# First norm computed by token, first gate unit tile by tile, first loads issued by two engines, and three shifts of convolution tile 2 moved from the matrix engine to the vector engine

## The reference, cut to what matters

```python
h = rmsnorm(x, norm_mix[0])                     # x * rsqrt(mean(x*x) + 1e-6) * g
a = jnp.einsum("bsd,de->bse", h, w_pw1) + b_pw1 # 1024 -> 2048
u = a[..., :d] * jax.nn.sigmoid(a[..., d:])     # value half, gate half
u = causal_dwconv(u, w_dw, b_dw)                # depthwise, 31 taps
u = jax.nn.silu(layernorm(u, ln_g, ln_b))
x = x + jnp.einsum("bsd,de->bse", u, w_pw2) + b_pw2
```

## Time and profile before

| | before |
|---|---|
| executions shown | 951.72, 952.87, 952.91 us, median 952.87 |
| the profiled execution's own time | 952.73 us, with a span of 950.9 us |
| mean granted TensorE clock | 0.994 of full speed |
| busy, share of the span | PE 938.1 us (99%), DVE 554.9 (58%), ACT 388.6 (41%), POOL 112.7 (12%) |
| instructions | 11880 |
| HBM read, written | 86.09 MB, 2.10 MB |

### The profile page before, as it was taken

How to read it: one execution, slowest core, us unless ns; L and a number is a source line. 1 busy time by engine, 2 the same in 40 slices (tenths; PEclk the granted TensorE clock), 3 DMA queues, 4 the chain that set the end, 5 groups by cost and what they waited for, 6 DMA issues and landing times.

```text
span 950.9 us, 11880 instructions
## 1 busy us (share of the span) xinstructions
PE 938.1 (99%) x4496; PEld 790.2 (83%) x4496; DVE 554.9 (58%) x711; ACT 388.6 (41%) x597; POOL 112.7 (12%) x74
## 2 busy tenths in 40 slices
PE   8999999999999999999999999999999999999996
PEld 6889898888888888888888898888888888888886
DVE  6899995657555555564434459765555555532333
ACT  7785596434334333342322355433343333322220
POOL 0558896000000000000000020000000000000000
PEclk9999999999999999999999999999999999999998
DMA  7320022232222223312222341232222232222212
GB/s 254 114 89 1 1 90 89 89 99 109 103 88 88 88 88 102 118 61 91 87 96 91 117 155 45 94 124 91 88 88 88 90 111 80 83 86 104 91 62 89
DMA packets 17020, 88.56 MB, mean 93 GB/s; under 512 B 2016, under 2 KB 4320, under 8 KB 9952
## 3 DMA queue, kind: packets, MB, share of 16 engines
q1 hardware_dynamic: 16416, 87.67, 27.0%
q10 hardware_dynamic: 576, 0.52, 0.2%
HBM read 86.09 MB, written 2.10 MB: 93 GB/s over the span
## 4 chain that ended last, share of the span: by engine, by line
PE 97%; DVE 1%; DMA 1%; ACT 0%; SPq 0%; issue 0%; DVEq 0%
PE bank L1127 29%; PE bank L1128 28%; PE bank L1129 28%; PE bank L1178 2%; PE bank L1180 2%; PE bank L1179 2%; PE bank L1469 1%; DMA x_res<-x 1%; DVE out_sb L1117 1%; PE bank L1196 0%; PE bank L1437 0%; PE bank L1442 0%; PE bank L1441 0%; PE bank L1202 0%; PE bank L1240 0%; PE bank L1230 0%
## 5 line engine op out<-in xcount | busy, mean ns | idle before, releaser
L1127 PE MATMUL bank<-h_hi,w_hi 128*128 128x512 f32 x800 | 312.4, 390 | 0.0
L1129 PE MATMUL bank<-h_hi,w_lo 128*128 128x512 f32 x800 | 311.4, 389 | 0.0
L1128 PE MATMUL bank<-h_lo,w_hi 128*128 128x512 f32 x800 | 311.3, 389 | 0.0
L455 ACT ACTIVATE w_hi<-w_raw 128x2048 fp32r<-128x2048 f32 (+2 forms) x87 | 147.3, 1693 | 211.9 <-PE bank L1129 211.9
L764 DVE TENSOR_TENSOR w_lo<-w_raw,w_hi 128x2048 fp32r<-128x2048 f32 (+2 forms) x81 | 162.1, 2002 | 100.6 <-ACT w_hi L455 99.8
L1127 PEld LDWEIGHTS bank<-h_hi,w_hi 128*128 128x128 f32 x800 | 150.2, 188 | 31.7 <-issue 0.5
L1128 PEld LDWEIGHTS bank<-h_lo,w_hi 128*128 128x128 f32 x800 | 150.2, 188 | 31.6 <-issue 0.5
L1129 PEld LDWEIGHTS bank<-h_hi,w_lo 128*128 128x128 f32 x800 | 150.2, 188 | 31.1
L1128 PE MATMUL bank<-u_lo,w_hi 128*128 128x512 f32 (+1 forms) x406 | 153.3, 378 | 0.0
L1127 PE MATMUL bank<-u_hi,w_hi 128*128 128x512 f32 (+1 forms) x374 | 141.1, 377 | 0.4 <-DVE w_lo L764 0.4
L1129 PE MATMUL bank<-u_hi,w_lo 128*128 128x512 f32 (+1 forms) x374 | 140.8, 377 | 0.0
(11 more groups left out here) (208 smaller groups left out, 996.1 us busy)
## 6 DMA issues: line engine op xcount, KB each, us to landing
w_raw<-w_up SPq DMA_DIRECT2D x44, 1024.0 KB, 4.8
w_raw<-w_down SPq DMA_DIRECT2D x32, 704.0 KB, 4.1
w_raw<-w_pw SPq DMA_DIRECT2D x11, 1024.0 KB, 4.9
x_res<-x SPq DMA_DIRECT2D x3, 512.0 KB, 8.0
out<-out_sb SPq DMA_DIRECT2D x12, 128.0 KB, 1.8
w_raw<-w_pw SPq DMA_DIRECT2D x4, 256.0 KB, 7.7
w_raw<-w_pool SPq DMA_DIRECT2D x2, 512.0 KB, 3.5
band_raw<-band SPq DMA_DIRECT2D x1, 800.0 KB, 5.5
```

The lines of the kernel that those rows point to most:

```text
L455: nc.scalar.activation(w_hi[s][:, 0:columns], w_raw[s][:, 0:columns], ACT.Copy).then_inc(w_rounded[s], 1)
L1127: M.matmul(dst, a, hi, start=start, stop=False)
L1128: M.matmul(dst, a, lo, start=False, stop=False)
L1129: return M.matmul(dst, b, hi, start=False, stop=stop)
```

## The change

- **Loads.** ACT now issues x tiles 0, 2 and 3 (as three loads of one tile; 2 and 3 were one load before) and parts 2 and 3 of unit 0; SP keeps `par`, parts 0 and 1, x tile 1, tiles 4 and 5, 6 and 7, unit 1 and the rest.
- **First norm.** The eight squares are added as a tree of five instructions (two of them 1024 columns wide). PE sums by blocks (`sum_wide`), ACT takes the root of four columns, DVE inverts four columns, and PE spreads the factors over the partitions (`spread_blocks`) into bank 5, from where ACT copies them to `rms`.
- **Second unit.** `second_unit` finishes gate tile 0 first, then gate tile 1, with the sum and the spread inside the latter. DVE drains and multiplies tile by tile.
- **Moved work.** The split of unit 0 of step 1 goes from DVE to POOL, the pool vectors from DVE to POOL, and ACT's `tap_columns` behind the first two sigmoids. `clear_sums` at the start is gone.
- **Tile 2.** The first `SOONER_SHIFTS` = 3 shifts of tile 2 become six taps on DVE (the last of 256 columns), added to the tile by one instruction; PE leaves them out of units 0 and 1. `conv_unit(2)` and one sum of POOL wait for that addition.
- **Order on DVE.** The numbers of taps between the drains are changed.

```diff
+SOONER_TILE, SOONER_SHIFTS, BANK_SOONER = 2, 3, 1
...
             sp.dma_start(par[:, 0:N_FIRST], vecs[:, 0:N_FIRST]).then_inc(par_loaded, 16)
-            load_x(0, 0, 1)
             load_part(0)
             load_x(1, 1, 2)
-            load_x(2, 2, 4)
             load_part(1)
-            load_x(3, 4, 6)
-            load_part(2)
-            load_part(3)
-            load_x(4, 6, 8)
+            load_x(4, 4, 6)
+            load_x(5, 6, 8)
...
-            pool.wait_ge(w_split[0], M_PW1 + 2)
+            pool.wait_ge(summed, KD + 1)
+            split(0, M_PW1 + 1)
+            split(1, M_PW1 + 1)
...
+            load_x(0)
             act.wait_ge(consts_set, CONSTS)
-            nc.scalar.activation(warm[:, :], eps[:, 0:1], ACT.Copy)
+            nc.scalar.activation(warm[:, 0:1], eps[:, 0:1], ACT.Copy)
+            load_x(2)
+            load_x(3)
+            load_part(2)
+            load_part(3)
...
+            touch_root()
+            act.wait_ge(stat_mm, 1)
+            nc.scalar.activation(root_tok[:, :], bank[BANK_SUM][:, 0:T:P], ACT.Sqrt, scale=1.0 / D, bias=eps[:, 0:1]).then_inc(root_done, 1)
+            nc.scalar.activation(warm[:, 1:2], eps[:, 0:1], ACT.Sigmoid)
...
+            act.wait_ge(first_spread, 1)
+            nc.scalar.activation(rms[:, :], bank[BANK_FIRST][:, :], ACT.Copy).then_inc(first_read, 1)
+            first_sigmoid(0)
+            first_sigmoid(1)
+            round_unit(1, M_PW1 + 1, UNIT)
             tap_columns()
-            round_unit(1, M_PW1 + 1, UNIT)
-            sigmoid(0)
...
-            add_square(0)
-            add_square(1)
             split_unit(1, M_PW1, UNIT)
-            for c in range(2, KD):
-                add_square(c)
-            split_unit(0, M_PW1 + 1, UNIT)
-            inverse(0)
+            add_squares(0)
+            add_squares(1)
+            dve.wait_ge(in_added, 4)
+            V.tensor_tensor(sumsq[:, :], in_sq[:, 0, :], in_sq[:, 4, :], ADD).then_inc(summed, KD + 1)
+            dve.wait_ge(root_done, 1)
+            V.reciprocal(root_tok[:, :], root_tok[:, :]).then_inc(rms_ready, 1)
...
             scale_val(3)
-            taps(1, 8, 15)
+            taps(1, 8, 13)
             drain_gate(3)
-            taps(1, 15, 16)
+            taps(1, 13, 14)
             multiply(3)
...
-            taps(1, 16, 24)
+            taps(1, 14, 24)
...
+                if u == 2:
+                    pe.wait_ge(sooner_added, 1)
+                first = {SHARED_TILE: SHARED_SHIFTS, SOONER_TILE: SOONER_SHIFTS}.get(CONV_TILES[n], 0)
...
+            def second_unit():
+
+
+                pe.wait_ge(w_rounded[1], 1)
+                for t in range(2):
+                    dst = bank[BANKS_PW1[0][1] + t][:, :]
+                    for k in range(KD):
+                        if (t, k) == (1, 1):
+                            pe.wait_ge(summed, KD + 1)
+                            sum_wide(sumsq, start=True, stop=True).then_inc(stat_mm, 1)
+                        if (t, k) == (1, 5):
+                            pe.wait_ge(ident_loaded, 16)
+                            pe.wait_ge(rms_ready, 1)
+                            spread_blocks(bank[BANK_FIRST], root_tok, range(BLOCKS)).then_inc(first_spread, 1)
```

More of the change, by code:

```diff
@@ L92 @@
 BANK_SUM, BANK_MEAN = 4, 7
+BANK_FIRST = 5
 BANK_IDLE = 3
@@ L145, in build @@
         pool_shift = place("pool_shift", [P, KD], f32)
-        warm = place("warm", [P, 1], f32)
+        warm = place("warm", [P, 2], f32)
         start_sum = place("start_sum", [P, START], f32)
@@ L888, in _ @@
+            dve.wait_ge(first_read, 1)
+            dve.wait_ge(first_gate, 1)
+            first_gate_drain(0)
+            scale_val(0)
+            first_multiply(0)
+            tap(0, 0, 0)
+            tap(0, 0, 1)
+            dve.wait_ge(unit_done[1], 1)
+            first_gate_drain(1)
+            tap(0, 0, 2)
+            first_multiply(1)
+            for k in range(3):
+                tap(0, 1, k)
+            taps(0, 3, 8)
             scale_val(1)
-            taps(0, 8, 13)
+            taps(0, 8, 15)
@@ L890, in _ @@
             drain_gate(1)
-            taps(0, 13, 15)
+            taps(0, 15, 17)
             multiply(1)
-            taps(0, 15, 20)
+            taps(0, 17, 21)
             scale_val(2)
-            taps(0, 20, 24)
+            taps(0, 21, 28)
             drain_gate(2)
-            taps(0, 24, 26)
+            taps(0, 28, 30)
             multiply(2)
-            taps(0, 26)
-            taps(1, 0, 8)
+            taps(0, 30)
+            for k in range(2 * SOONER_SHIFTS):
+                sooner_tap(k)
+                taps(1, k, k + 1)
@@ L1241, in first_unit @@
                 last.then_inc(unit_done[0], 1)
-            def first_norm(k):
-                if k == 5:
-                    sum_channels(0)
+            def second_unit():
[10 more added lines that the diff above has]
+                            spread_blocks(bank[BANK_FIRST], root_tok, range(BLOCKS)).then_inc(first_spread, 1)
+                        a = w_hi[1][:, (2 * k + t) * P:(2 * k + t + 1) * P]
+                        M.matmul(dst, a, h_hi[:, k, :], start=k == 0, stop=False)
+                        M.matmul(dst, a, h_lo[:, k, :], start=False, stop=False)
+                    pe.wait_ge(w_split[1], 1)
+                    for k in range(KD):
+                        last = M.matmul(dst, w_lo[1][:, (2 * k + t) * P:(2 * k + t + 1) * P], h_hi[:, k, :], start=False, stop=k == KD - 1)
+                    last.then_inc(first_gate if t == 0 else unit_done[1], 1)
             def second_norm(k):
@@ L1282, in wait_free @@
                     wait_drained((2, 3), DRAINED_PW1 + {(2, 0): 1, (3, 1): 3}[i, s])
-            for i in range(PW1_STEPS):
-                for s in range(0 if i else 1, 2):
+            second_unit()
+            for i in range(1, PW1_STEPS):
+                for s in range(2):
                     wait_free(i, s)
-                    unit(s, M_PW1 + i, h_hi, h_lo, None if i else first_norm, at_bank=BANKS_PW1[i][s])
+                    unit(s, M_PW1 + i, h_hi, h_lo, at_bank=BANKS_PW1[i][s])
                 if i == 2:
```

93 lines of the change are left out of this document (61 added, 32 removed).

## The result

The changed kernel takes 955.58 us (median; 954.64 to 956.76 over 7 runs), the kernel before 952.31 us beside it (951.72 to 953.05). The ratio is 1.0035, 95% interval 1.0026 to 1.0044: **slower by 0.35%, 3.3 us**. The forecast was 951.9 us with a range up to 954.0 us, so it was wrong in size and in sign. The profiled execution of the changed kernel took 954.98 us, 2.25 us more than the profiled one of before.

The account below looks back on a forecast made before the run. PE was taken to bound the kernel, DVE close behind. The start's 1.05 and tile 2's 2.14 make 3.2 us, 2.3 given back on DVE: 0.9 gained, 951.9 us; own range 951.0 to 952.6, with rivals 950.2 to 954.0.

Parts of the forecast that it names:

- I take 16.0 us: Start: unit 1's load, which landed at 16.56 before, would land at 16.0 us; forecast range 15.1 to 16.6.
- path two: Start: unit 1's landing, ACT's rounding, DVE's split and adds lead to the sum over channels, issued at 24.9 us.
- The start gives 1.05 us: Start: `second_unit` would end at 31.7 us instead of 32.75, a gain of 1.05 us.
- My first rival: Start: loads come no earlier and PE's stall stays; sum at 26.8 us, total 953.9 us, slower; 20%.
- The second norm of the start: In `second_unit`: behind the sum's issue come 22 matmuls (5.0 us), the sum (0.9) and the spread (0.9).
- tile 2: Mixer: 18 matmuls of 256 columns leave PE, a gain of 2.14 us.
- DVE's load: Mixer: with its added taps DVE is ready near 105.1 and waits 1.5 us at the last gate drain.
- Four taps have moved behind that drain: 2.64 us ... 0.35 slack: Last gate drain to layer norm: 2.64 us more DVE work less 0.35 slack gives back 2.3 of 3.2 us.
- The clock falls in the layer norm: Layer norm: two new PE waits of 1.1 and 1.2 us lower the clock, costing 1.65 us, 953.6 us; 13%.

Follow-up runs that it names:

- experiment 1: The changed kernel with all first loads issued by SP again, in the order of before: 953.47 us, ratio 1.0018 to the kernel before.
- experiment 6: The changed kernel with one tap pair back ahead of the last gate drain, mean from PSUM, parts 2 and 3 on SP ahead of unit 1: 949.59 us.
- experiment 7: The kernel before with only the change's loads (ACT issues x tiles 0, 2, 3 and parts 2, 3): 954.46 us, ratio 1.0025.
- experiment 12: The kernel before with only x tiles 0, 2 and 3 issued by ACT, parts 2 and 3 staying on SP ahead of unit 1: 951.95 us, ratio 1.0001.
- experiment 2: The changed kernel with one pair of taps moved back ahead of the last gate drain: 955.12 us, ratio 1.0032 to the kernel before.
- experiment 3: The changed kernel with the shared tile's first tap reading the near mean from PSUM instead of SBUF: 952.81 us, ratio 1.0006 to the kernel before.
- experiment 9: The changed kernel with 14 and 7 idle matmuls ahead of PE's two new waits at the end of the mixer: 955.55 us, ratio 1.0033.
- experiment 10: The changed kernel with 8 and 4 idle matmuls ahead of PE's two new waits at the end of the mixer: 954.50 us, ratio 1.0023.
- experiment 8: The kernel before with only the mean taken from PSUM by the shared tile's first tap: 951.80 us, ratio 0.9996.
- experiment 5: The changed kernel with first loads as before, one tap pair back ahead of the last gate drain, and the mean from PSUM: 950.18 us, ratio 0.9979.

## Why the prediction was wrong

**"I take 16.0 us" for the landing of unit 1, and the step that hangs the sum on that landing alone: these failed.** Unit 1 landed at 16.55, inside the range of 15.1 to 16.6. The larger miss is that I took path two to be landing, rounding, split, adds, and left out that ACT must first round part 3 of unit 0 and x tiles 6 and 7 and square two tiles. The change had just moved part 3 into another queue, and I priced ACT's issues and the bytes of unit 1, not the landing of the small load beside it. Part 3 landed at 15.27, and ACT came to unit 1 1.5 us after its landing; the sum was issued at 26.90 instead of 24.9. Of these 2.0 us the landing is 0.55 and the wait for ACT the rest. "The start gives 1.05 us" became a loss of 1.0: 2.05 us. Experiments 1, 6, 7 and 12 show it from four sides, among them that 24.7 to 25.5 is what the same chain gives when part 3 is on time.

My first rival had the right sign and nearly the right moment of the sum (26.8 us; its total of 953.9 was 1.7 short), but another mechanism: it had PE's stall stay. So that moment was met by luck: the stall shrank, and PE waited for DVE. The Trainium skill (page "DMA: Bandwidth & Descriptors", section "Issuing engines are not separate DMA queues"), which spoke against this term, was right for unit 1, which was issued 3.4 us sooner and landed at 16.55 as before. Single loads did move: ACT rounded x tile 2 at 8.46 instead of 9.65, and x tile 1 at 7.83 instead of 5.82. The section's word that such transfers interleave is the sharper warning, and the same page's section on queues, rings and completion order says that an SDMA engine takes turns between the rings it has work for. The runs agree with that: part 3 in a queue beside x tiles 4 to 7 and unit 1 landed 11.83 us after its issue (11.2 in experiment 7), and ahead of unit 1 in one queue after 8.8 (9.0 in experiment 12).

**The second norm of the start, tile 2 and DVE's load: right.** `second_unit` itself costs what was reckoned: from the sum to the next unit 6.94 us, predicted 6.8. PE gained 2.14 less the start's loss. DVE had 1.22 us of idle time at the last drain (predicted 1.5), and the wide add took the 1.22 us taken for it.

**"Four taps have moved behind that drain: 2.64 us ... 0.35 slack": right, but not all of it.** The step treats DVE's other instructions behind the drain as unchanged. One of them waits for POOL, and the same change had shifted DVE against POOL: +0.93 us. The 1.48 us of this one tap among taps of 0.75 stood in the trace of before, and I had not asked what they were. Experiments 2 and 3 show the cause. The Trainium skill (page "SBUF — State Buffer", section "SBUF: two separate sides") states it: VectorE and GpSimd share a port pair, and a DVE instruction with two SBUF inputs and a GpSimd one that reads SBUF shut each other out for the whole instruction. The trace agrees: DVE's end stands 0.55 or 0.56 us behind POOL's in all eight kernels that keep this form (before, the change, experiments 1, 2, 7, 9, 10 and 12), wherever it began. It shows the other side too: POOL's work next behind it takes 4.08 us before, where the same takes 3.62 in experiment 8.

**"The clock falls in the layer norm": it did**, a rival with 13%. Its sign and place were right. The price of 1.65 us is not refuted: in the profiled execution of the change the stretch from the sum of squares to that of `conv_out` took 0.69 more and the maximum 0.45 less, but in experiment 1 that stretch took 1.4 more, and in experiment 2 it is 44.87 us from the last drain to the end of the maximum, 2.4 more than in the change. The wait that set it off was 1.92 us instead of 1.1, for the DVE wait had been added to it; in experiment 3, with 0.44 and 0.93, the clock held.

Missed as well, in the change's favour: the maximum with zero, 0.45 us less, which the slow clock brought with it. The four misses are 2.05 + 0.93 + 0.69 - 0.45 = 3.2 us, which is the distance between the -0.9 forecast and the +2.3 found. The cases were also treated as rivals of one another, where two of them came together with a third that had no case. That, more than any width, put 955.6 outside a range that ended at 954.0.

## What to carry to other kernels

When a small load moves to a second queue, ask what loads then run beside it, and which instruction stands behind the small one on its consumer; keep what is needed first ahead in the same queue. An instruction that takes twice its neighbours' time is a wait with a cause, and its length changes when either engine moves. A stall is worth only what the next wait leaves of it, and a wait that is free now may not stay so: DVE's for POOL cost nothing in the kernel before, and taking it away gave 2.8 us by the medians once DVE was last.

## What the runs showed that was not expected

- A DVE instruction with two SBUF tensors in fp32 takes 1.48, 2.41 or 3.79 us in place of 0.75, according to how long POOL's running instruction still lasts. With one of the two in PSUM it takes 0.75 beside the same POOL instruction.
- A DVE TENSOR_SCALAR on 4 columns shows the same: 0.62 us when it ended with POOL's split (148.81 and 148.78), 0.17 where it began within 0.1 us of that split's end or behind it. It has one tensor input, in place, in SBUF. No run here was made to test it.
- A small load in a second queue can pay for it: 256 KB took 11.83 us to land beside x tiles 4 to 7 and 1 MB in the other queue, and 8.8 us ahead of that 1 MB in one queue.
- A 128-column fp32 matmul of ones is two records of 0.11 us, so 0.22 us of filling and not 0.11.
- The same wait of PE for `rest_sum` (1.90 to 1.92 us) was followed by slow stretches of different lengths. From the sum of squares to the end of the maximum it is 4.24 us before, 4.46 in the change, 5.35 in experiment 1 and 6.81 in experiment 2.
- The start differs from run to run. The same order of loads had unit 1 rounded at 15.89 and at 16.67 us (experiments 1 and 5), and the nine runs of experiment 7 spread over 2.7 us.
